# Down projection of a decoder layer: four of eight row blocks by seven products, with the sums of weights formed on GpSimd

## The reference, cut to what matters

```
h = rmsnorm(x, norm_ffn_g[l])
x = x + jnp.square(jax.nn.relu(h @ w_up[l])) @ w_down[l]
```

## Time and profile before

| | before |
|---|---|
| median of three runs | 1522.63 us (1522.37 to 1523.03) |
| the profiled execution's own time | 1521.96 us |
| its span, first to last instruction | 1519.9 us |
| PE busy | 1505.6 us, 99% |
| DVE busy | 1190.9 us, 78% |
| ACT busy | 756.1 us, 50% |
| POOL busy | 2.0 us, 11 instructions |
| mean granted TensorE clock | 0.998 |

### The profile page before, as it was taken

How to read it: one execution, slowest core, us unless ns; L and a number is a source line. 1 busy time by engine, 2 the same in 40 slices (tenths; PEclk the granted TensorE clock), 3 DMA queues, 4 the chain that set the end, 5 groups by cost and what they waited for, 6 DMA issues and landing times. The chain is left out here.

```text
span 1519.9 us, 22403 instructions
## 1 busy us (share of the span) xinstructions
PE 1505.6 (99%) x7670; PEld 1270.0 (84%) x7670; DVE 1190.9 (78%) x1578; ACT 756.1 (50%) x942; POOL 2.0 (0%) x11
## 2 busy tenths in 40 slices
PE   9999999999999999999999999999999999999997
PEld 8888888877778888888888888888888888888885
DVE  6568888988889877565556779987798779887798
ACT  5544444465554455444445445545455545544553
POOL 0000000000000000000000000000000000000000
PEclk9999999999999999999999999999999999999999
DMA  7655566655556556656555655655656565566553
GB/s 240 194 180 190 187 195 199 196 182 173 171 171 193 194 194 211 194 195 199 181 180 171 197 186 208 207 190 170 207 190 211 170 211 199 181 196 203 204 198 138
DMA packets 209961, 290.86 MB, mean 191 GB/s; under 512 B 9227, under 2 KB 129107, under 8 KB 209778
## 3 DMA queue, kind: packets, MB, share of 16 engines
q1 hardware_dynamic: 209906, 290.14, 58.2%
HBM read 287.48 MB, written 2.10 MB: 191 GB/s over the span
## 5 line engine op out<-in xcount | busy, mean ns | idle before, releaser
L503 ACT ACTIVATE w_hi<-w_raw 128x1024 fp32r<-128x1024 f32 x510 | 532.8, 1056 | 458.0 <-PE acc L1321 266.2
L729 DVE TENSOR_TENSOR w_lo<-w_raw,w_hi 128x1024 fp32r<-128x1024 f32 x510 | 614.6, 1221 | 170.6 <-ACT w_hi L503 165.8
L1297 PE MATMUL acc<-h_hl,w_hi 128*128 128x512 f32 x1740 | 546.7, 395 | 0.0
L1295 PEld LDWEIGHTS acc<-h_hl,w_lo 128*128 128x128 f32 x1740 | 322.3, 188 | 72.7 <-issue 0.6
L1295 PE MATMUL acc<-h_hl,w_lo 128*128 128x256 f32 x1740 | 343.6, 279 | 0.0
L1297 PEld LDWEIGHTS acc<-h_hl,w_hi 128*128 128x128 f32 x1740 | 265.2, 189 | 0.0
L1319 PE MATMUL acc<-w_hi,m_hl 128*128 128x512 f32 x456 | 177.8, 390 | 0.0
L1321 PE MATMUL acc<-w_hi,m_hl 128*128 128x512 f32 x456 | 177.4, 389 | 0.0
L1320 PE MATMUL acc<-w_lo,m_hl 128*128 128x512 f32 x456 | 177.4, 389 | 0.0
L1319 PE MATMUL acc<-w_hi,h_hl 128*128 128x512 f32 x384 | 151.5, 394 | 0.0
L1321 PE MATMUL acc<-w_hi,h_hl 128*128 128x512 f32 x384 | 149.6, 389 | 0.0
(11 more groups left out here) (202 smaller groups left out, 1472.8 us busy)
## 6 DMA issues: line engine op xcount, KB each, us to landing
w_raw<-in_w_in SPq DMA_DIRECT2D x200, 512.0 KB, 3.5
w_raw<-in_w_up SPq DMA_DIRECT2D x128, 512.0 KB, 4.3
w_raw<-in_w_down SPq DMA_DIRECT2D x128, 512.0 KB, 4.4
w_raw<-in_w_mix_out SPq DMA_DIRECT2D x32, 512.0 KB, 3.6
w_raw<-in_w_sconv_out SPq DMA_DIRECT2D x16, 512.0 KB, 4.2
w_raw<-in_w_attn_out SPq DMA_DIRECT2D x16, 512.0 KB, 3.9
w_raw<-in_w_conf_out SPq DMA_DIRECT2D x16, 512.0 KB, 4.2
bias_row<-in_gate_b SPq DMA_DIRECT2D x12, 256.0 KB, 3.9
```

What stands on the lines that cost most here:

```text
L503: act.activation(w_hi[:, q], w_raw[:, q], ACT.Copy).then_inc(hi_done, 1)
L729: dve.tensor_tensor(w_lo[:, q], w_raw[:, q], w_hi[:, q].bitcast(F32), ALU.subtract).then_inc(lo_done, 1)
L1295: pe.matmul(*narrow[m], start=False, stop=False)
L1297: last = pe.matmul(*wide[m], start=False, stop=final)
```

## The change

Six things change.

1. A trip has quads at k = 4, 6, 10 and 12 (4, 6 and 10 in the very last trip): 31 in all where there were 23. The order of the slabs changes with them, and an ordinary pair of slabs stands at the end of each trip.
2. `forms_first` and `forms_second` move from DVE to GpSimd, which now runs a loop of its own over the down trips.
3. `w_forms` becomes two buffers, used in turn. Space for the second comes from joining the attention buffers. `w_sums` stays one buffer.
4. T1 and T3 are rounded first, one iteration ahead of T2 and T4; PE takes the products in an order that follows.
5. SP gets a new wait: a slot of the ring that held a quad is loaded again only when GpSimd has made that quad's sums (`t_raw`).
6. The sums at the end of a trip are split over k = 13, 14 and 15, and `WARM_GAP` goes from 20 to 6.

```diff
-PAIR = [(0, 0), (0, 1), (1, 0), (1, 1), (0, 2), (1, 2), (0, 3), (1, 3), (0, 4), (1, 4), (0, 5), (1, 5)]
-PAIR_ENDS = {False: [(0, 6), (1, 6), (0, 7), (1, 7)], True: [(0, 6), (0, 7), (1, 6), (1, 7)]}
+ROWS_FIRST = [(0, 0), (0, 2), (1, 0), (1, 2), (0, 1), (1, 1), (0, 3), (1, 3), (0, 4), (1, 4), (0, 5), (1, 5)]
+ROWS_LAST = {False: [(0, 7), (1, 7), (0, 6), (1, 6)], True: [(0, 6), (0, 7), (1, 6), (1, 7)]}
...
-    return (6, 10) if last_trip(ph, c, t) else (6, 10, 14)
+    return (4, 6, 10) if last_trip(ph, c, t) else (4, 6, 10, 12)
...
-WARM_GAP = 20
+WARM_GAP = 6
...
+                if ph.name in ("up", "down"):
+                    summed = c * (2 * PAIR_QUADS * PH["down"].trips) + (t * (2 * PAIR_QUADS) if ph.name == "down" else 0)
+                    held = [x for x in quads(ph, c, t) if k - RING in (x, x + 1)]
+                    if held:
+                        sp.wait_ge(t_raw, quad_of(ph, c, t, held[0]) * 2 + 2)
+                    elif k < 2 and not (isinstance(summed, int) and summed == 0):
+                        sp.wait_ge(t_raw, summed)
...
+            def forms_first(ph, c, t, k):
+
+                x, y = k % RING, (k + 1) % RING
+                quad = quad_of(ph, c, t, k)
+                if not (isinstance(quad, int) and quad == 0):
+                    pool.wait_ge(t_lo, quad * 2 - 1)
+                pool.wait_ge(raw_full[x], raw_count(ph, c, t, k))
+                pool.wait_ge(raw_full[y], raw_count(ph, c, t, k + 1))
+                left = w_raw[:, x:x + 2, 0:2, :].rearrange("p s k b -> p s (k b)")
+                pool.tensor_tensor(w_sums[:, T1:T3 + 1, :], wide_rows(w_raw[:, y]), left, ALU.subtract).then_inc(t_raw, 1)
+
+            def forms_second(ph, c, t, k):
+
+                x, y = k % RING, (k + 1) % RING
+                quad = quad_of(ph, c, t, k)
+                pool.wait_ge(t_raw, quad * 2 + 1)
+                if not (isinstance(quad, int) and quad == 0):
+                    pool.wait_ge(t_lo, quad * 2)
+                pool.tensor_tensor(w_sums[:, T2, :], half_rows(w_raw[:, y], 1), w_sums[:, T1, :],
+                                  ALU.subtract).then_inc(t_two, 1)
+                pool.wait_ge(t_two, quad + 1)
+                pool.tensor_tensor(w_sums[:, T4, :], half_rows(w_raw[:, x], 1), w_sums[:, T2, :],
+                                  ALU.subtract).then_inc(t_raw, 1)
...
                 if k + 2 in quads(ph, c, t):
-                    act.wait_ge(t_raw, quad_of(ph, c, t, k + 2) * 2 + 2)
-                    act.activation(w_forms[:, 0, 2:4, :], w_sums[:, 2:4, :], ACT.Copy).then_inc(t_hi, 1)
+                    act.wait_ge(t_raw, quad_of(ph, c, t, k + 2) * 2 + 1)
+                    act.activation(w_forms[quads(ph, c, t).index(k + 2) % 2][:, 0, 0:2, :], w_sums[:, 0:2, :], ACT.Copy).then_inc(t_hi, 1)
                 if k + 1 in quads(ph, c, t):
-                    act.activation(w_forms[:, 0, 0:2, :], w_sums[:, 0:2, :], ACT.Copy).then_inc(t_hi, 1)
+                    act.wait_ge(t_raw, quad_of(ph, c, t, k + 1) * 2 + 2)
+                    act.activation(w_forms[quads(ph, c, t).index(k + 1) % 2][:, 0, 2:4, :], w_sums[:, 2:4, :], ACT.Copy).then_inc(t_hi, 1)
...
-                    if k + 3 in quads(ph, c, t):
-                        forms_second(ph, c, t, k + 3)
-                    if ph.name == "down" and k == 15 and not last_trip(ph, c, t):
-                        corner_sums(c, t)
+                    if ph.name == "down" and k == 14 and not last_trip(ph, c, t):
+                        corner_sums(c, t, 0, slab_of(ph, c, t, k))
                     lo(ph, c, t, k)
-                    if k + 4 in quads(ph, c, t):
-                        forms_first(ph, c, t, k + 4)
...
+                        if k == 13:
+                            products_in(c, t, s)
                         if k == 15:
-                            token_sums(c, t, s)
+                            corner_sums(c, t, 1, s)
+                            products_on(c, t)
```

More of the change, by code:

```diff
@@ L133, in quads @@
         return ()
[L134 removed]
+    return (4, 6, 10) if last_trip(ph, c, t) else (4, 6, 10, 12)
 def quad_of(ph, c, t, k):
[L139 removed]
+    return c * (4 * PH["down"].trips) + t * 4 + quads(ph, c, t).index(k)
 def pair_of(c, t):
@@ L484, in _, with trip @@
                                fill=MASKED, base=-1, pattern=[[1, BLK]], channel_multiplier=-1).then_inc(consts, 1)
+            def forms_first(ph, c, t, k):
[18 more added lines that the diff above has]
+                                  ALU.subtract).then_inc(t_raw, 1)
+            def trip(ph, c, t):
+                for k in quads(ph, c, t):
+                    forms_first(ph, c, t, k)
+                    forms_second(ph, c, t, k)
+            trip(PH["down"], 0, 0)
+            with pool.Fori(1, PH["down"].trips) as t:
+                trip(PH["down"], 0, t)
+            with pool.Fori(1, CHUNKS - 1) as c:
+                with pool.Fori(0, PH["down"].trips) as t:
+                    trip(PH["down"], c, t)
+            for t in range(PH["down"].trips):
+                trip(PH["down"], CHUNKS - 1, t)
         @block.scalar
@@ L742, in forms_second @@
[L742 to L751, removed]
@@ L753, in forms_lo @@
             def forms_lo(ph, c, t, k, part):
                 dve.wait_ge(t_hi, quad_of(ph, c, t, k) * 2 + part + 1)
-                two = slice(2, 4) if part == 0 else slice(0, 2)
-                dve.tensor_tensor(w_forms[:, 1, two, :], w_sums[:, two, :], w_forms[:, 0, two, :].bitcast(F32),
+                two = slice(0, 2) if part == 0 else slice(2, 4)
+                both_parts = w_forms[quads(ph, c, t).index(k) % 2]
+                dve.tensor_tensor(both_parts[:, 1, two, :], w_sums[:, two, :], both_parts[:, 0, two, :].bitcast(F32),
@@ L1329, in products_quad @@
                 quad, first, final = quad_of(ph, c, t, k), k == quads(ph, c, t)[0], k == quads(ph, c, t)[-1]
-                closing = final and not last_trip(ph, c, t)
                 w_x, w_y = k % RING, (k + 1) % RING
+                both_parts = w_forms[quads(ph, c, t).index(k) % 2]
                 def whole(b, kt):
@@ L1363, in products_quad @@
                 product(P_BANK["P1"], whole(0, 2 * i), loaded(w_x, 0), first, final).then_inc(slab_used, 1)
+                pe.wait_ge(lo_done, s + 2)
+                pe.wait_ge(f_lo, c * 4 + i // 2 + 1)
+                product(6, form(S4), loaded(w_y, 1), False, False)
+                pe.wait_ge(t_lo, quad * 2 + 1)
+                product(P_BANK["P7"], form(S3), summed(T3), first, final)
+                product(P_BANK["P5"], form(S1), summed(T1), first, final)
+                pe.wait_ge(t_lo, quad * 2 + 2)
                 product(P_BANK["P6"], form(S2), summed(T2), first, final)
-                pe.wait_ge(t_lo, quad * 2 + 2)
-                product(P_BANK["P7"], form(S3), summed(T3), first, final)
-                product(P_BANK["P5"], form(S1), summed(T1), first, final).then_inc(slab_used, 1)
+                product(5, whole(1, 2 * i + 1), summed(T4), False, False).then_inc(slab_used, 1)
             def transposed(dst, src):
```

94 lines of the change are left out of this document (40 added, 54 removed).

## The result

The changed kernel takes 1622.27 us (median of 4 runs, 1620.94 to 1622.35), the one before 1522.50 (4 runs, 1521.79 to 1523.03): 1.0655 times as long, interval 1.0642 to 1.0669. That is 99.8 us more. The forecast was 1545, with a range to 1574: slower, but by more than four times what it said.

The account below looks back on a forecast made before the run. The prediction held TensorE to be the bound, running without a gap in down trips, with VectorE close behind. It summed 1522.6 - 7.4 (gains) + 30 (VectorE and GpSimd blocking each other) = 1545 us, range 1513 to 1574.

Parts of the forecast that it names:

- turns: Down trips: SBUF reads of GpSimd and two-input VectorE instructions block each other; the likeliest case, chance 0.50, 1530 to 1575.
- the gains: On TensorE: 5.4 us from 24 dropped matmuls and 2.0 from the earlier beginning, 7.4 us in all.
- the start: Fewer warm-up matmuls let real work begin 2.0 us earlier, at 10.3 instead of 12.32; bounds nothing and 2.4.
- I take turns ... and of their price 30 us, between 22 and 39: Down trips: the step that chose mutual blocking of VectorE and GpSimd and added 30 us for it.
- The chain: Down trips: loads and TensorE wait for slow GpSimd sums while VectorE runs undisturbed; a rival, chance 0.15.
- S: Time of one quad's sums on GpSimd: 4.7 us taken, 6.5 if slowed by VectorE.
- the 5.5: Limit in us for a quad's sums on GpSimd, under which TensorE would lose nothing.
- 21 us: Loss in seven down trips when a quad's sums on GpSimd take 6.5 us, at 3 us a trip per us over.
- the select's: GpSimd's rate from its 128-element select, 2.28 ns an element, giving 4.7 us a quad.
- a lead of 4.3 us: VectorE's lead over TensorE at each of four chunks, eaten first; takes 17 us off the price of blocking.
- The 39 us: Price of full blocking in seven ordinary down trips: 46.4 us of VectorE and GpSimd work in 40.8, 5.6 too many.
- 73 us: Price of full blocking if VectorE's 4.9 us a trip on PSUM never fell beside GpSimd; kept as a bound.

Follow-up runs that it names:

- fills_beside: The kernel before, plus GpSimd fills and one-element subtractions four times a down trip that nobody waits for: 1522.31 us, 1.0001.
- one_element: The changed kernel, but GpSimd's three sums of a quad cover one element each (first quad whole): 1517.57 us, 0.9972.
- gap6: The kernel before with WARM_GAP 6 in place of 20 and nothing else: 1521.02 us, 0.9993.
- sums_on_dve: The changed kernel with all four quads' sums moved back to VectorE: 1542.22 us, 1.0137.
- three_dve: The changed kernel with three quads a trip, at k = 4, 6 and 10, and their sums on VectorE: 1534.89 us, 1.0087.
- fills: The changed kernel with GpSimd's sums replaced by three constant fills each, reading only single elements: 1644.59 us, 1.0806.
- reads_idle: The changed kernel with one-element sums, plus five GpSimd additions on idle buffers behind each quad that nobody waits for: 1564.61 us, 1.0279.
- fills_short: The changed kernel with GpSimd's sums replaced by two constant fills each, reading only single elements: 1579.28 us, 1.0376.
- three_late_dve: The changed kernel with quads at k = 6, 10 and 12 (6 and 10 in the last trip), sums on VectorE: 1522.15 us, 0.9994.

## Why the prediction was wrong

**Right.** The sign, and the mechanism named for it. The changed kernel shows the signs that the forecast set for turns: rests of 2035 and 1686 ns where it asked for 1500 or more, and waits of more than 3 us in a trip. Its third sign, a 1024-element sum over 2300 ns, came true at 3171 but could not tell: the first sum, which was not held up, took 2620 as well. The section Who interferes with whom of the page "SBUF — State Buffer" of the Trainium skill says that the later of the two waits until the other is through; the trace agrees, with 2.42 us for a 0.29 us instruction, and the 1.0001 of fills_beside bears out that it is a matter of GpSimd's reads. The forecast also had about right the gains (7.4 us in the sum; one_element is 4.7 under the kernel before and its one real quad costs 3.2 of wait, 7.9 together) and the start (first real matmul expected at 10.3, seen at 10.53, clock held), though gap6 can't show the start's 2.0 us in the whole time. A fourth quad with the sums on VectorE does cost: sums_on_dve is 7 us slower than three_dve.

**Wrong: the step "I take turns ... and of their price 30 us, between 22 and 39".** The loss over one_element is 1622.3 - 1517.6 = 105 us, where the step had 30. Four things are in it that the step left out or had too small.

*The chain was made a rival and not a term.* The forecast worked out that S would grow to 6.5 by turns, "over the 5.5", and priced that, at 21 us, only in a case in which VectorE runs undisturbed. But turns bring lateness with them, and both are paid. By the line of fills, S = 7.47 without any blocking gives 1579.3 + 0.33 x 28.9 = 1589, which is 71 us over one_element. That leaves some 33 us that lateness doesn't explain, with VectorE's own instructions slowed. Reads that nobody waits for, in reads_idle, give 47, with some lateness of their own in it, as said above; 71 and 47 together are 14 over the 105. So either the two overlap or reads_idle counts lateness twice. Neither figure alone reaches 105.

*S was too small.* The sums took 2.6 + 1.4 + 1.3 = 5.3 us alone, about 2.6 ns an element, not the select's 2.28 (4.7 us). In turns S was 7.47 (5.35 to 8.47), not 6.5. The figure of 4497 ns for 2048 elements in the GPSIMD Engine Reference of the Trainium skill, section 3.1, gave an estimate of 4.8 for the three together, which is too short as well; the measurement decides. With its gaps the quad at the start took 5.5 us (907.02 to 912.55), already over the point where the loss begins, which was near 4.6 and not 5.5. So even GpSimd free of VectorE would have lost; as an estimate, at S = 5.5 the fills' points give 1532 (the line carried down) to 1542 (straight from the first point to the second), 14 to 25 us over one_element.

*The lead was gone at once.* The forecast let each chunk eat a lead of 4.3 us first, 17 us in all. In the first down trip TensorE already stood 3.20 us at slab 3, ahead of the first quad's products, because VectorE's small instructions had been held up. Behind the free part a microsecond of S costs 28.9 us in all, some 3.7 a trip, where the forecast's rival had 3.

*No turn fell beside VectorE's PSUM work.* The 39 us presume that GpSimd's reads use the time in which VectorE works on PSUM. In the changed kernel none did: that work stands at the end of a trip, and GpSimd was through with the trip's sums by then. The forecast's own figure for this case was 73 us. Nor was VectorE "at 90% of such a trip" after the change; 32.6 of 40.8 us is 80%, and the 90% is that of the kernel before.

**The clock had no price.** The forecast asked about it only at the start. In the down trips 26.3 us of the loss are matmuls that start 0.3 to 0.55 us apart, and 22 us of that lie in stretches with a granted clock of 0.50, the 1.2 GHz level. The down trips have 14 such stretches (before: none), each behind a stall of TensorE of 2.3 to 4.3 us from start to start, as the window 916 to 920 behind the 3.2 us. That stalls cause it is argued from this order; no run held the clock up while the stalls stayed. It is part of the 105, not beside it, and the experiments' slopes contain it too (granted clock 0.991 in fills_short, 0.977 in fills).

What the forecast had in hand came closer than what it chose: the 73 us of turns that never fall beside VectorE's PSUM work, with 21 for the chain, would have made 94 - 7.4 and a time of 1609. It set the 73 aside as a bound and the 21 as another case. That this sum comes near is partly luck, since S, its price and the clock were each too low in it.

**Open.** How the 105 us divide between blocking and lateness is known only roughly, as reads_idle has both in it, and what part late loads have in the stalls wasn't separated. The chain's own length behind one slot was not varied (a deeper ring of `w_raw` wasn't tried). No version beat the kernel before: gap6 and three_late_dve are level with it, and one_element leaves the sums out.

## What to carry to other kernels

Before work is moved from VectorE to an idle GpSimd, look at what both read: if VectorE is busy with two-input instructions on SBUF for most of the stretch, each of GpSimd's reads can stop it for its whole length and be stopped by it, and GpSimd's help can be dearer than leaving the sums on VectorE (100 us against 20 over the kernel before, here). GpSimd's writes alone cost nothing here (ratio 1.0001), and VectorE instructions with an input in PSUM ran on undisturbed. When a slowed step is also on a chain with little slack, the blocking and the lateness are both paid, and the stalls cost TensorE's clock on top; don't put them in separate cases. Measure slack with fills of growing length before trusting a hand-made sum of leads, and in a test of "reads that nobody waits for" see that the next real work on that engine isn't queued behind them.

## What the runs showed of the hardware that was not expected

The price of GpSimd's reads differed much: 209 us of them cost 125 us beside the kernel before, where VectorE has three quads' sums of its own, and 228 us cost 47 us where it has none. That the fuller VectorE makes the difference is likely but not isolated; the sizes and places of the reads differ too. Stalls of 2.3 to 4.3 us in a dense stream of matmuls were each followed by some microseconds at the 1.2 GHz level (0.50 in the window 916 to 920); the slower matmuls there make 22 of the 100 us. A one-element subtraction on GpSimd took 0.19 us at the least, and 0.36 (fills) to 0.70 us (line 508 of one_element) on the average beside VectorE.
